# Modulation scale before shift, and the query product on scaled tokens, in a hybrid GLA/Hyena/MoE layer

## The chip, the cores and the metric

The kernel runs on one core of a Trainium2 chip. The metric is the device time in microseconds of one execution. Everything is float32.

## The reference, cut to what matters

One layer for a prompt of 128 tokens and a denoising sample of 256 tokens (384 tokens, width 2048). The first stage is the one that changes:

```python
mod = silu(cond) @ w_ada + b_ada            # w_ada: 2048 x 12288, two condition vectors
sh1, sc1, gt1, sh2, sc2, gt2 = split(mod, 6)
h = rmsnorm(x, g_pre_mix) * (1 + sc1) + sh1
proj = h @ w_in                             # columns: q 512, k 512, v 1024, g 1024, lr 32, Hyena 3072
la   = log_sigmoid(lr @ w_dec + b_dec) / 16 # decays of the gated linear attention, two directions
```

After that come gated linear attention over four heads, two long convolutions (Hyena), the output projection, a second norm and modulation with sh2 and sc2, a router, and sixteen experts of which each token uses two.

## The kernel before, in words

Each engine runs one fixed instruction list, written out by hand, and engines meet at semaphores. SyncE (SP) issues nearly all weight loads in one order; a load that waits for its buffer holds every later one back.

**Modulation.** `ada_step` (L439) takes 16 loads of 2 MB, each 128 rows of w_ada over the 4096 columns of shift and scale together, through three ring slots (`next_slot`, L333). It multiplies them by the silu of the conditions (`sT`) on four column groups of TensorE (L450). In between, `x_turn` (L456) transposes the normed tokens, and ScalarE copies them to `hT` (L1256). Then VectorE adds the bias row (`mod_row`, L1562), TensorE turns the row into columns (`mod_columns`, L479), and VectorE applies scale and shift to `hT` in 32 instructions (L1623), after which `project("q")` starts (L503, matmuls of 384 columns; L506 is the same function for 512).

**The order behind it.** q, the low-rank product lr (L532), eight decay products `la` (L541, each read by ScalarE at L1271 and by VectorE at L1632), k, v0, v1, the transposes of the decayed keys (L552), g0, g1, then six Hyena blocks, and the output projection. Every projection has two halves of one 2 MB load each.

**The other four rows of the modulation** are computed by VectorE, in pieces. A piece is 256 rows by 512 columns, loaded as two DMAs of 256 KB into the third ring slot, cut in four (`piece_view`). `run(n)` on VectorE works off n half pieces of two instructions each (L1587 for the first of a chunk, L1592 else). There are 16 chunks of 16 half pieces. When a chunk is complete, TensorE sums it over the partitions (`ada_sum`, L432) at the end of the projection half that the table `ADA_SUMS` names, and VectorE adds it to its row (`mod_chunk`, L1554). `PIECES_AFTER` says how many pieces SP loads behind which weight load; piece n waits until piece n-4 has been used.

**Where VectorE and TensorE meet.** Before the first attention head VectorE has run 136 half pieces: run(26), the eight decay rows L1632, run(4), the decay sums (L1640 to L1647), mod_chunk(0), run(14), the products with q and k (L1654 to L1659, "ks"), then mod_chunk(1), run(20), mod_chunk(2), run(16), mod_chunk(3), run(16), mod_chunk(4), run(20), mod_chunk(5), run(16), mod_chunk(6), run(4), mod_chunk(7). TensorE's side of a head (`gla_updates`, L564) is woven into the second half of g1. It writes a state update into one PSUM bank per direction and, before it writes the next, waits until VectorE has read the last (L1685, L1687).

Of the kernel before, what the change touches and what calls it, by code (L numbers as in the profile page):

```python
# [20 lines left out]
P = 128  # L21
D = 2048
# [39 lines left out]
def shape_constants():  # L62
# [15 lines left out]
    base = np.concatenate([ident, tri, sel.reshape(P, 2 * P), total, np.tile(rows, (P, 1)), tokens, lower], 1).astype(np.float32)  # L78
# [55 lines left out]
def build(nc, T):  # L134

    ctx = ExitStack()
    with ctx:
# [17 lines left out]
        base = sb("base", [P, 4 * P + 32 + N_ROWS + NT + 1])  # L155
# [5 lines left out]
        colA = sb("colA", [P, 50])  # L161
# [18 lines left out]
        second_half = base[:, at_row + N_ROWS + NT:at_row + N_ROWS + NT + 1]  # L180
        ps = ctx.enter_context(nc.psum_tensor("ps", [P, 8, NCOL], F32))
# [20 lines left out]
        rowsA = region(25856, P, rows=50)  # L202
# [36 lines left out]

        wr = at(AT_GAIN, KT, 32)  # L240
# [89 lines left out]
        def slot_view(slot):  # L330
            return ring_mem[:, SLOT * slot:SLOT * (slot + 1)]
# [19 lines left out]
        def w_block(w, row0, col0):  # L351
# [9 lines left out]
        ADA_BANK = 6  # L361
        ADA_KEYS = ["ada0", "ada1", "ada2", "ada3", "ada4", "ada5"]
# [4 lines left out]
        PIECES_AFTER = {1: 8, 2: 8, 3: 3, 4: 6, 5: 4, 6: 7, 7: 7, 8: 8, 9: 9, 10: 7, 11: 5, 12: 4, 13: 6, 14: 4,  # L367
                        15: 6, 16: 4, 17: 8, 18: 2, 20: 2, 22: 2, 24: 2, 25: 4, 27: 4, 28: 6, 29: 2}
# [38 lines left out]
        def _(pe):  # L407
# [4 lines left out]
            pe.wait_ge(S("in_rowsA"), 16 * 6)  # L412
            take(pe, 5, "colA")
            tr(ps[:, 5, 0:50], rowsA, ident[0:50, 0:50]).then_inc(filled("colA"), 1)
            pe.wait_ge(S("in_rowsB"), 32)
            take(pe, 4, "colB")
            tr(ps[:, 4, 0:96], rowsB, ident[0:96, 0:96]).then_inc(filled("colB"), 1)

            pe.wait_ge(S("in_mlp"), 16 * 9)
            take(pe, 3, "hid1")  # L420
            mm(ps[0:HID, 3, 0:TOK], w1s, pe_sb, start=True, stop=True).then_inc(filled("hid1"), 1)

# [14 lines left out]
            ada_at = [0]  # L437

            def ada_step():  # L439


                third, k = divmod(ada_at[0], KT)
                ada_at[0] += 1
                w = next_slot(pe, w_ada[k * P:(k + 1) * P, third * SLOT:(third + 1) * SLOT])
                for n in range(8):
                    bank, j = ADA_BANK + n // 4, n % 4
                    key = ADA_KEYS[third * 2 + n // 4]
                    if k == 0 and j == 0:
                        take(pe, bank, key)
                    m = mm(ps[32 * j:32 * j + 32, bank, :], sT[:, k, :], w[:, n, :], start=(k == 0),  # L450
                           stop=(k == KT - 1), skip_group_check=True)
                    if k == KT - 1 and n == 3:
                        m.then_inc(filled(key), 1)
                slot_done(m, key if k == KT - 1 else None)
# [8 lines left out]
            pe.wait_ge(S("sT_ready"), 2)  # L463
            for k in range(KT):
                ada_step()
                if k == KT - 8:
                    pe.wait_ge(S("hid_ready"), 1)
                    take(pe, 3, "hid2")
                    mm(ps[:, 3, 0:TOK], w2s, ftmp[0:HID, 1, :], start=True, stop=True).then_inc(filled("hid2"), 1)
                    pe.wait_ge(S("x_scaled"), NT)  # L470
                if KT - 8 <= k < KT - 1:
                    for kt in range(3 * (k - KT + 8), min(KT, 3 * (k - KT + 8) + 3)):
                        x_turn(kt)

# [6 lines left out]

            wait_read(pe, "dve", ADA_KEYS[0])
            mod_columns(0, 2)
            pe.wait_ge(S("mod_ready"), 1)
            mod_columns(1, 3)

            def project_half(key, kind, w, col0, kh, readers=("act",), between=None, banks=(0, 1, 2, 3),
# [4 lines left out]
                for m_ in range(n):  # L492
# [3 lines left out]
                    if m_ == 2 and between:  # L496
                        between()
                    for k in range(8):
                        kk = kh * 8 + k
                        if key == "q" and m_ == 0:  # L500
                            pe.wait_ge(S("h_modulated"), kk + 1)
# [24 lines left out]
            project("q", "fm", w_in, COL_Q)  # L526

            pe.wait_ge(S("in_lr"), 16)
            take(pe, 4, "lr", ("act",))
            for k in range(KT):  # L530
                j = k % 4
                m = mm(ps[32 * j:32 * j + 32, 4, 0:TOK], wlr[:, k, :], hT[:, k, :], start=(k < 4), stop=(k >= KT - 4),  # L532
                       skip_group_check=True)
            m.then_inc(filled("lr"), 1)

            wait_read(pe, "act", "lr")
            pe.wait_ge(S("in_dec"), 128)
            for d in range(2):
                for h in range(HEADS):
                    take(pe, 4 + h % 2, f"la{d}{h}", ("act", "dve"))  # L540
                    mm(ps[:, 4 + h % 2, 0:TOK], wdec[:, d, h * DK:(h + 1) * DK], lrT,  # L541
                       start=True, stop=True).then_inc(filled(f"la{d}{h}"), 1)
            project("k", "fm", w_in, COL_K)
# [192 lines left out]
            pe.wait_ge(S("mod_ready"), 3)  # L736
# [229 lines left out]
        def _(sp):  # L966

            def small_loads():
                sp.dma_start(rowsA[0:16, :], T["c_ctx"].rearrange("(k p) -> k p", p=P)).then_inc(S("in_rowsA"), 16)
# [5 lines left out]
                sp.dma_start(base[:, :], T["k_base"]).then_inc(S("in_base"), 16)  # L975

            pieces = [0]
# [13 lines left out]
            for i, (slot, src) in enumerate(loads):  # L991
# [66 lines left out]
        def _(pool):  # L1058
# [5 lines left out]
            g.op(nc.gpsimd.memset(wdec, 0.0), S("wdec_zero"))  # L1064
# [73 lines left out]
            pool.wait_ge(S("mod_ready"), 2)  # L1138
# [11 lines left out]
            pool.wait_ge(S("mod_ready"), 4)  # L1150
            pool.dma_start(prompt_gate.rearrange("o (j n) -> (o j) n", j=4), mod[0:P:32, 5, :]
                           ).then_inc(S("prompt_gate_row"), 16)
# [6 lines left out]
            pool.dma_start(br[:, NG:NG + NE], T["b_router_exp"].broadcast_to([P, NE])).then_inc(S("in_router"), 16)  # L1159

# [46 lines left out]
        def _(act):  # L1207
# [6 lines left out]

            load(rowsB[0:72, :], T["hy_conv_w"][0].rearrange("j (m p) -> (j m) p", p=P), "in_rowsB")
# [7 lines left out]
            for t in range(NT):  # L1223
                load(x_sb[:, t, :], x_rows[t], "in_x")
# [5 lines left out]

            act.wait_ge(S("sin_arg"), 1)
            a.op(A(ftmp[0:HID, 1, :], ftmp[0:HID, 0, :], ACT.Sin), S("hid_ready"))
# [12 lines left out]
            act.wait_ge(S("in_x"), 16 * NT)  # L1245
            for t in range(NT):
                squares(x_sb[:, t, :], h_tm[:, t, :], t)
            act.wait_ge(S("eps_ready"), 1)
            roots(0, NT, D)
            act.wait_ge(S("sin_arg"), 2)  # L1250
            a.op(A(hdn[:, :], ftmp[:, 0, :], ACT.Sin), S("hdn_ready"))

            def h_columns(name):
                for kt in range(KT):
                    b = read(act, f"{name}{kt}")
                    a.op(A(hT[:, kt, :], ps[:, b, 0:TOK], ACT.Copy), freed("act", f"{name}{kt}"))  # L1256

            h_columns("xT")
# [4 lines left out]

            for m_ in range(4):
                copy_out(f"q_{m_}", qf[:, m_, :])
# [242 lines left out]
        def _(dve):  # L1508
# [13 lines left out]
            v.op(ve.tensor_copy(colA[:, :], ps[:, b, 0:50]), freed("dve", "colA"))  # L1522
            b = read(dve, "colB")
            v.op(ve.tensor_copy(colB[:, :], ps[:, b, 0:96]), freed("dve", "colB"))
# [19 lines left out]
            dve.wait_ge(S("in_mlp"), 16 * 9)  # L1544
            sine_argument("hid1", 0, HID)

            def mod_chunk(m):

                if m == 0:
                    dve.wait_ge(S("in_rows"), 16 * 10)  # L1550
# [6 lines left out]
            def mod_row(q):  # L1557

                dve.wait_ge(S("in_rows"), 16 * 10)
                if q < 2:  # L1560
                    b = read(dve, ADA_KEYS[q])
                    v.op(ve.tensor_tensor(mod[:, q, :], mod[:, q, :], ps[:, b, :], ALU.add), freed("dve", ADA_KEYS[q]))  # L1562
                if q % 3 == 0:
                    return
# [575 lines left out]
```

## Time and profile before

| what | value |
|---|---|
| time, median of 3 runs | 1530.26 us (1526.99 to 1530.33) |
| the profiled execution: its time, its span | 1530.56 us, 1528.7 us |
| TensorE (PE) matmul busy | 1379.7 us, 90% |
| VectorE (DVE) busy | 748.8 us, 49% |
| ScalarE (ACT) busy | 241.7 us, 16% |
| DMA | 422.19 MB, mean 276 GB/s |
| chain that ended last | PE 74%, DMA 11%, DVE 8% |

TensorE, VectorE and DMA in 40 slices of 38 us (tenths of busy time; PEclk is the granted TensorE clock):

```profile
PE   2679999999999989999999999889989888798977
DVE  0139889998677687978693752530000000000006
PEclk9689999999999999999999999989999999999999
DMA  9998458777549643322215844589999999999996
```

The first three slices are the modulation. Up to slice 25 the layer's body follows, and behind it the experts, in which DMA is at nine tenths. One matmul of float32 leaves two records in the trace, so a projection half of 32 matmuls of 384 columns shows as 64 records.

### The profile page before, as it was taken

To read this page: it belongs to the slowest core of one execution; us is meant where nothing else is said; L and a number is where in the kernel's file an instruction comes from. 1 tells how busy PE (TensorE), PEld (TensorE's weight loads), DVE (VectorE), ACT (ScalarE), POOL (GpSimd) and SP (SyncE) were. 2 spreads that over 40 slices of the span, in tenths; PEclk is the share of its full clock that TensorE was granted. 3 is DMA by queue.
4 is the path that set the end of the run, shared out by engine and by line. 5 is a ranking of instruction groups with operands and counts; after the bars stand their busy time and mean duration, and the time that the engine had idled before them with its cause. 6 is when DMAs were issued, how large, how long until landed. Compare 5 with 4: busy or idle time off the path is not lost.

```text
span 1528.7 us, 14045 instructions
## 1 busy us (share of the span) xinstructions
PE 1379.7 (90%) x5198; PEld 630.9 (41%) x5198; DVE 748.8 (49%) x1269; ACT 241.7 (16%) x401; POOL 75.1 (5%) x126
## 2 busy tenths in 40 slices
PE   2679999999999989999999999889989888798977
PEld 0135544444555545555544444543333333333322
DVE  0139889998677687978693752530000000000006
ACT  2110320100011111211121101521111101111104
POOL 3010000000001000000000001000000000000001
PEclk9689999999999999999999999989999999999999
DMA  9998458777549643322215844589999999999996
GB/s 345 424 359 254 170 173 276 249 259 254 165 144 339 222 146 109 117 69 90 83 55 213 289 157 170 235 351 427 427 426 394 430 427 428 426 386 427 427 424 279
DMA packets 134032, 422.19 MB, mean 276 GB/s; under 512 B 10253, under 2 KB 76024, under 8 KB 116852
## 3 DMA queue, kind: packets, MB, share of 16 engines
q1 hardware_dynamic: 120292, 375.79, 64.3%
q0 software_dynamic: 7584, 33.38, 6.0%
q10 hardware_dynamic: 6096, 12.20, 2.2%
q8 instruction: 40, 0.66, 0.2%
q14 instruction: 20, 0.16, 0.0%
HBM read 407.96 MB, written 22.58 MB: 282 GB/s over the span
## 4 chain that ended last, share of the span: by engine, by line
PE 74%; DMA 11%; DVE 8%; issue 3%; ACT 2%; ACTq 0%; POOL 0%; DVEq 0%; SPq 0%; POOLq 0%
PE ps L503 19%; PE ps L506 19%; PE ps L892 13%; PE ps L912 7%; DMA s_mem<-in_w_exp_gate 4%; PE ps L777 3%; DMA s_mem<-in_w_ada 3%; DMA s_mem<-in_w_exp_down 2%; DVE s_mem L1766 2%; PE ps L450 2%; PE ps L674 1%; DMA s_mem<-in_hy_freq 1%; PE ps L625 1%; PE ps L432 1%; DVE s_mem L1738 1%
## 5 line engine op out<-in xcount | busy, mean ns | idle before, releaser
L1592 DVE SCALAR_TENSOR_TENSOR s_mem<-s_mem,s_sT 128x512 f32<-128x512 f32 x480 | 339.4, 748 | 32.6 <-DMA s_mem<-in_w_ada 16.2
L503 PE MATMUL ps<-s_mem 128*128 128x384 f32 x1024 | 342.5, 492 | 1.1 <-DVE s_mem L1623 1.1
L506 PE MATMUL ps<-s_mem 128*128 128x512 f32 x672 | 292.8, 594 | 0.7 <-ACT s_mem L1366 0.7
L892 PE MATMUL ps<-s_mem 128*64 128x512 f32 x1152 | 256.4, 602 | 19.9 <-DMA s_mem<-in_w_exp_gate 18.7
L503 PEld LDWEIGHTS ps<-s_mem 128*128 128x128 f32 x1024 | 193.3, 191 | 142.5 <-issue 18.0
L506 PEld LDWEIGHTS ps<-s_mem 128*128 128x128 f32 x672 | 126.3, 190 | 158.5 <-issue 157.6
L892 PEld LDWEIGHTS ps<-s_mem 128*64 128x64 f32 x1152 | 87.4, 139 | 185.9 <-issue 185.9
L2059 DVE TENSOR_TENSOR s_mem<-s_mem,ps 64x512 f32<-64x512 f32 x18 | 12.2, 679 | 296.3 <-ACT s_mem L1461 296.3
L912 PE MATMUL ps<-s_mem 128*64 128x512 f32 x576 | 144.2, 659 | 9.3 <-DVE s_mem L2061 9.3
L1262 ACT ACTIVATE s_mem<-ps 128x512 f32<-128x512 f32 (+1 forms) x61 | 34.4, 581 | 316.3 <-PE ps L506 154.0
L912 PEld LDWEIGHTS ps<-s_mem 128*64 128x64 f32 x576 | 43.7, 150 | 96.4 <-issue 84.6
L2066 DVE COPY s_mem<-ps 128x512 f32<-128x512 f32 x18 | 12.4, 691 | 141.9 <-PE ps L912 141.9
L450 PE MATMUL ps<-s_mem,s_sT 128*32 128x512 f32 x256 | 43.2, 815 | 20.5 <-DMA s_mem<-in_w_ada 20.5
L1461 ACT ACT_TABLE_LOAD x17 | 21.8, 1283 | 241.0 <-PE ps L892 241.0
L625 PE MATMUL ps<-s_mem 128*128 128x512 f32 x96 | 42.9, 596 | 0.7 <-ACT s_mem L1262 0.7
L777 PE MATMUL ps<-s_mem 128*128 128x512 f32 x96 | 41.5, 592 | 0.0
L902 PE MATMUL ps<-s_base,s_mem 64*128 64x64 f32 x72 | 11.9, 285 | 30.9 <-DVE s_mem L2059 30.9
L1466 ACT ACTIVATE s_mem<-ps 128x512 f32<-128x512 f32 x18 | 10.7, 596 | 155.1 <-PE ps L912 155.1
L1307 ACT ACTIVATE s_mem<-ps,s_colB 128x384 f32<-128x384 f32 x24 | 16.1, 670 | 118.5 <-PE ps L503 118.5
L1893 DVE TENSOR_TENSOR s_mem<-s_mem,ps 128x512 f32<-128x512 f32 x12 | 7.9, 684 | 48.0 <-PE ps L777 25.1
L1347 ACT ACTIVATE s_mem<-s_mem 128x512 f32<-128x512 f32 x24 | 14.5, 630 | 93.5 <-DVE s_mem L1751 93.5
L450 PEld LDWEIGHTS ps<-s_mem,s_sT 128*32 128x32 f32 x256 | 8.3, 134 | 49.3 <-DMA s_mem<-in_w_ada 30.6
(287 smaller groups left out, 1025.0 us busy)
## 6 DMA issues: line engine op xcount, KB each, us to landing
s_mem<-in_w_ada SPq DMA_DIRECT2D x256, 256.0 KB, 3.2
s_mem<-in_w_exp_gate SPq DMA_DIRECT2D x32, 2048.0 KB, 21.1
s_mem<-in_w_exp_up SPq DMA_DIRECT2D x32, 2048.0 KB, 25.4
s_mem<-in_w_exp_down SPq DMA_DIRECT2D x32, 2048.0 KB, 24.4
s_mem<-in_w_in SPq DMA_DIRECT2D x24, 2048.0 KB, 8.8
s_mem<-in_w_ada SPq DMA_DIRECT2D x16, 2048.0 KB, 12.5
s_mem<-in_w_out SPq DMA_DIRECT2D x8, 2048.0 KB, 8.2
y_slots<-s_mem ACTq DMA_DIRECT2D x34, 256.0 KB, 11.1
```

What stands on the lines that cost most here:

```text
L450: m = mm(ps[32 * j:32 * j + 32, bank, :], sT[:, k, :], w[:, n, :], start=(k == 0), stop=(k == KT - 1), skip_group_check=True)
L503: m = mm(ps[:, banks[m_], 0:TOK], v[:, k, m_ * P:(m_ + 1) * P], hT[:, kk, :], start=(kk == 0), stop=(kk == KT - 1))
L506: m = mm(ps[:, banks[m_], :], hT[:, kk, m_ * P:(m_ + 1) * P], v[:, k, :], start=(kk == 0), stop=(kk == KT - 1))
L625: mm(ps[:, bank, :], dft[:, table, :], src, start=True, stop=True).then_inc(filled(key), 1)
L777: m = mm(ps[:, bank, :], hT[:, kh * 8 + k, t * P:(t + 1) * P], last_w[kh][:, k, :], start=(kh + k == 0), stop=(kh * 8 + k == KT - 1))
L892: m = mm(ps[half, 0, :], hgT[:, kh * 8 + k, :], weights(e, 2 * kh + which)[:, k, :], start=(kh + k == 0), stop=(kh * 8 + k == KT - 1), ski ...
L912: m = mm(ps[half, 4 + n // 2, :], heT[:, 2 * kh + k, :], weights(e, 4 + kh)[:, k, n * NCOL:(n + 1) * NCOL], start=(kh + k == 0), stop=(kh ...
L1262: a.op(A(dst, ps[:, b, 0:n], func), freed("act", key))
L1307: a.op(A(hyT[:, m_, :], ps[:, b, 0:TOK], ACT.Identity, bias=colB[:, 72 + c:73 + c], scale=colB[:, 24 + c:25 + c]), freed("act", key))
L1461: A(sg, ps[BLK:2 * BLK, 0, :], ACT.Silu).then_inc(S("sg_ready"), 1)
L1592: v.op(ve.scalar_tensor_tensor(out=o, in0=w, scalar=scale, in1=o, op0=ALU.mult, op1=ALU.add), S("piece_used") if last else None)
L1766: v.op(ve.reciprocal(temps[4 + s], ps[:, b, :]), freed("dve", f"norm{ho}{s}"))
```

## The change

Scale and shift are computed one behind the other. The scale comes in eight loads (two halves of 1024 columns, four loads each), then the shift in eight loads of 2048 columns. The tokens are multiplied by the scale only, q is computed on these while the shift's loads arrive, and the shift's part of q (shift times W_q) is computed as a row and added by ScalarE as a bias. The shift is then added to `hT` (32 VectorE instructions, as before) for the other projections. There are four ring slots in this stage, and both halves of W_q have buffers of their own. x is loaded ahead of the small tensors. The lr product moves behind the first half of k, and the decay products stand between the parts of k's second half.

```diff
-            slot = i % RING if i < KT else (i - KT + 1) % 2
+            slot = (0, 1, 2, 3, 0, 1, 2, 3, 0, 1, 2, 3, 0, 1, 3, 0)[i] if i < KT else (i - KT + 1) % 2
...
-        ADA_SUMS = {("q", 1): 0, ("k", 1): 1, ("v0", 1): 2, ("v1", 0): 3, ("v1", 1): 4, ("g0", 0): 5, ("g0", 1): 6,
-                    ("g1", 0): 7, ("g1", 1): 8, ("hy00", 1): 9, ("hy01", 1): 10, ("hy10", 0): 12,
-        PIECES_AFTER = {1: 8, 2: 8, 3: 3, 4: 6, 5: 4, 6: 7, 7: 7, 8: 8, 9: 9, 10: 7, 11: 5, 12: 4, 13: 6, 14: 4,
+        Q_LOAD_AFTER = {3: 0, 7: 1}
+        ADA_SUMS = {("k", 1): 0, ("v0", 1): 1, ("v1", 0): 2, ("v1", 1): 3, ("g0", 0): 4, ("g0", 1): 5, ("g1", 0): 6,
+                    ("g1", 1): 7, ("hy00", 0): 8, ("hy00", 1): 9, ("hy01", 1): 10, ("hy10", 0): 12,
+        PIECES_AFTER = {16: 4, 17: 8, 18: 3, 19: 2, 20: 6, 21: 6, 22: 8, 23: 8, 24: 11, 25: 11, 26: 7, 27: 7, 28: 5,
...
+            def scale_columns(h):
+                wait_read(pe, "act", f"scale{h}")
+                take(pe, 5, f"scaleT{h}")
+                for i in range(8):
+                    m = mm(ps[:, 5, 32 * i:32 * i + 32], scale_sums[:, i % 4 * P:(i % 4 + 1) * P], conds[:, i // 4, :], ...)
+            def q_products(m_, kts):
+                for kt in kts:
+                    if m_ == 0:
+                        pe.wait_ge(S("h_scaled"), kt + 1)
+                    m = mm(ps[:, m_, 0:TOK], wq[kt // 8][:, kt % 8, m_ * P:(m_ + 1) * P], hT[:, kt, :], ...)
+            scale_step(0, 0)
+            scale_step(0, 1)
+            pe.wait_ge(S("x_scaled"), NT)
+            for kt in range(KT):
+                x_turn(kt)
+                if kt in (4, 9):
+                    scale_step(0, 2 + kt // 9)
+            scale_columns(0)
...
+            for m_ in range(4):
+                take(pe, m_, f"q_{m_}", ("act",))
+                m = q_products(m_, range(8))
+                scale_step(1, m_)
+            m.then_inc(S("q_read"), 1)
+            shift_step(0)
+            scale_columns(1)
+            shift_step(1)
...
+            for m_ in range(4):
+                m = q_products(m_, range(8, 12))
+                if m_ % 2 == 1:
+                    shift_step(2 + m_ // 2)
+            m.then_inc(S("q_read"), 1)
+            for m_ in range(2):
+                q_products(m_, range(12, KT)).then_inc(filled(f"q_{m_}"), 1)
+                shift_step(4 + m_)
+            shift_step(6)
+            shift_step(7)
+            q_products(2, range(12, KT)).then_inc(filled("q_2"), 1)
+            wait_read(pe, "dve", "shift")
+            mod_columns(SHIFT, 5)
+            q_products(3, range(12, KT)).then_inc(filled("q_3"), 1)
+            # 16 matmuls of 512 columns on four column groups: shift columns times W_q -> "qshift"
...
-            project("q", "fm", w_in, COL_Q)
+            project_half(*where_k, 0, between=q_shift_columns, banks=(4, 5, 7, 0))
+            # lr, 16 matmuls as before, in bank 3
+            project_half(*where_k, 1, banks=(4, 5, 7, 0), turn=decay_products())   # two la behind each quarter
...
 VectorE:
-            run(26)
+            run(12)
             for d in range(2):
                 for h in range(HEADS):
                     ...  # L1632, as before
-            run(4)
+                    if h % 2 == 1 and (d, h) != (1, 3):
+                        run(3)
+            run(6)
...
+            run(10)
             mod_chunk(1)
-            run(20)
+            run(10)
             mod_chunk(2)
...
-                    run((2, 1, 2, 1, 1, 1, 2, 2)[event])
+                    run((2, 2, 2, 1, 1, 1, 2, 2)[event])
...
-            mod_chunk(7)
             gla_head(0)
-            mod_chunk(8)
+            mod_chunk(7)
             gla_head(1)
             wait_read(dve, "act", "g1_2")
+            mod_chunk(8)
```

## Rows read from the trace of the kernel before

**Rows 1.** Windows of the whole core: busy us (instructions), clock, DMA share, GB/s.

```profile
core 0: us, PE busy (x) PEld busy (x) DVE busy (x) ACT busy (x) POOL busy (x), PEclk, DMA share, GB/s
0.00:105.80 105.80, 55.17 (x318) 15.82 (x319) 13.22 (x27) 18.76 (x30) 13.04 (x25) 0.85 0.95 379
162.00:360.00 198.00, 196.72 (x545) 92.57 (x543) 179.03 (x248) 30.64 (x34) 1.09 (x2) 1.00 0.70 228
26.00:31.00 5.00, 5.00 (x29) 1.30 (x32) 2.83 (x6) 0.52 (x1) 0.00 (x0) 1.00 0.84 318
640.00:642.00 2.00, 2.00 (x6) 0.76 (x4) 1.97 (x6) 0.60 (x1) 0.00 (x0) 1.00 1.04 407
```

**Rows 2.** Chain that ended last, in order of time: start us, us, what.

```profile
84.89 13.95 DMA s_mem<-in_w_ada
98.89 3.64 PE ps L450 x16
105.83 43.15 PE ps L503 x128
```

**Rows 3.** Timeline, TensorE, from lr to the first head.

```profile
149.72 2.82 PE L532 MATMUL ps<-s_mem 128*32 128x384 f32 x30
158.00 1.53 PE L541 MATMUL ps<-s_mem 128*128 128x384 f32 x4 [0.84 <-DVE s_mem L1632]
161.74 41.44 PE L503 MATMUL ps<-s_mem 128*128 128x384 f32 x128
203.11 1.06 PE L432 MATMUL ps<-s_mem 128*32 128x256 f32 x8
204.10 41.47 PE L506 MATMUL ps<-s_mem 128*128 128x512 f32 x96
366.07 0.70 PE L564 MATMUL ps<-s_mem 64*128 64x256 f32 x4
```

**Rows 4.** Timeline, VectorE, from the decay rows to the first head.

```profile
139.87 13.28 DVE L1592 SCALAR_TENSOR_TENSOR s_mem<-s_mem,s_sT 128x512 f32<-128x512 f32 x18
159.61 1.26 DVE L1632 TENSOR_SCALAR s_mem<-ps,s_colA 128x384 f32<-128x384 f32 x2 [1.11 <-ACT s_mem L1271]
169.72 1.76 DVE L1640 TENSOR_TENSOR s_mem<-s_mem 128x1536 f32<-128x1536 f32 x1 [0.55 <-ACT s_mem L1278]
183.73 0.41 DVE L1554 TENSOR_TENSOR s_mem<-s_mem,ps 64x256 f32<-64x256 f32 x1
209.38 0.19 DVE L1654 COPY s_decs<-s_mem 128x24 f32<-128x24 f32 x1 [4.88 <-ACT s_mem L1285]
219.84 0.41 DVE L1554 TENSOR_TENSOR s_mem<-s_mem,ps 64x256 f32<-64x256 f32 x1
361.67 0.42 DVE L1554 TENSOR_TENSOR s_mem<-s_mem,ps 64x256 f32<-64x256 f32 x1
363.40 0.76 DVE L1685 COPY s_mem<-ps 128x256 f32<-128x256 f32 x2 [1.31 <-PE ps L564]
```

**Rows 5.** The page's list of DMA issues: size, median us to landing.

```profile
s_mem<-in_w_in SPq DMA_DIRECT2D x24, 2048.0 KB, 8.8
```

**Rows 6.** Timeline, TensorE, ScalarE and VectorE in the first stage.

```profile
31.26 1.91 ACT L1237 ACTIVATE s_mem<-s_mem 128x2048 f32<-128x2048 f32 x1 [1.51 <-DMA s_mem<-in_x_sample]
79.44 1.92 PE L450 MATMUL ps<-s_mem,s_sT 128*32 128x512 f32 x16
104.09 0.66 PE L479 MATMUL ps<-s_base,s_mem 128*128 128x128 f32 x4 [1.03 <-DVE s_mem L1568]
105.01 9.87 DVE L1623 TENSOR_SCALAR s_mem<-s_mem,s_modT 128x128 f32<-128x128 f32 x32
114.80 0.87 DVE L1587 TENSOR_SCALAR s_mem<-s_mem,s_sT 128x512 f32<-128x512 f32 x2
```

**Rows 7.** Who waited for whom, VectorE from 100 to 1000 us: total, times, longest.

```profile
DVE s_mem L1592 <- DMA s_mem<-in_w_ada: 16.2, 9, 5.5
```

More of the change, by code:

```diff
@@ L77, in shape_constants @@
     lower = (np.arange(P) >= BLK)[:, None]
-    base = np.concatenate([ident, tri, sel.reshape(P, 2 * P), total, np.tile(rows, (P, 1)), tokens, lower], 1).astype(np.float32)
+    shifts = np.zeros((P, 32), np.float32)
+    for j in range(4):
+        for c in range(2):
+            shifts[32 * j + 2 + c, c] = 1
+    conds = np.zeros((P, 2, 32), np.float32)
+    for j in range(4):
+        for c in range(2):
+            conds[32 * j + c, j // 2, c] = 1
+    base = np.concatenate([ident, tri, sel.reshape(P, 2 * P), total, np.tile(rows, (P, 1)), tokens, lower, shifts, conds.reshape(P, 64)], 1).astype(np.float32)
     masks = np.zeros((P, 2, P), np.int32)
@@ L435, in ada_sum, with scale_step, shift_step @@
                 mi.then_inc(filled(key), 1)
[L437 to L454, printed above, removed]
+            def scale_step(h, r):
+                cols = SCALE * D + 2 * h * NCOL
+                w = next_slot(pe, w_ada[4 * r * P:4 * (r + 1) * P, cols:cols + 2 * NCOL].rearrange("(k p) n -> p k n", p=P))
+                if r == 0:
+                    take(pe, 7 - h, f"scale{h}", ("act",))
+                for kk in range(4):
+                    k = 4 * r + kk
+                    for jj in range(2):
+                        j = 2 * jj + k % 2
+                        m = mm(ps[32 * j:32 * j + 32, 7 - h, :], sT[:, k, :], w[:, 2 * kk + jj, :], start=(k < 2),
+                               stop=(k >= KT - 2), skip_group_check=True)
+                slot_done(m, f"scale{h}" if r == 3 else None)
+            def shift_step(a):
+                w = next_slot(pe, w_ada[2 * a * P:2 * (a + 1) * P, SHIFT * D:(SHIFT + 1) * D].rearrange("(k p) n -> p k n", p=P))
+                if a == 0:
+                    take(pe, 7, "shift")
+                for k in (2 * a, 2 * a + 1):
+                    for j in range(4):
+                        m = mm(ps[32 * j:32 * j + 32, 7, :], sT[:, k, :], w[:, 4 * (k % 2) + j, :], start=(k == 0),
+                               stop=(k == KT - 1), skip_group_check=True)
+                slot_done(m, "shift" if k == KT - 1 else None)
             def x_turn(kt):
@@ L461, in x_turn @@
                 m.then_inc(filled(f"xT{kt}"), 1)
[L463 to L473, printed above, removed]
             def mod_columns(q, bank):
@@ new lines, in _ @@
+            wait_read(pe, "dve", "shift")
+            mod_columns(SHIFT, 5)
+            q_products(3, range(12, KT)).then_inc(filled("q_3"), 1)
+            wait_read(pe, "dve", "modT0")
+            take(pe, 6, "qshift", ("act",))
+            for k in range(KT):
+                j = k % 4
+                m = mm(ps[32 * j:32 * j + 32, 6, :], sT[:, k, :], wq[k // 8][:, k % 8, :], start=(k < 4),
+                       stop=(k >= KT - 4), skip_group_check=True)
+            m.then_inc(filled("qshift"), 1)
@@ L487, in project_half, with q_shift_columns @@
+            def q_shift_columns():
+                wait_read(pe, "act", "qshift")
+                take(pe, 6, "colQ", ("act",))
+                for m_ in range(4):
+                    m = mm(ps[:, 6, m_ * 32:m_ * 32 + 32], q_shift[:, m_ * P:(m_ + 1) * P], shift_rows, start=True,
+                           stop=True, skip_group_check=True)
+                m.then_inc(filled("colQ"), 1)
             def project_half(key, kind, w, col0, kh, readers=("act",), between=None, banks=(0, 1, 2, 3),
@@ L495, in project_half @@
                         take(pe, banks[m_], bk, readers)
-                    if m_ == 2 and between:
+                    if m_ == (1 if key == "k" else 2) and between:
                         between()
@@ L1212, in load @@
                 act.dma_start(dst, src).then_inc(S(sem), 16)
+            for t in range(NT):
+                load(x_sb[:, t, :], x_rows[t], f"in_x{t}")
             load(rowsB[0:72, :], T["hy_conv_w"][0].rearrange("j (m p) -> (j m) p", p=P), "in_rowsB")
@@ L1249, in _, with sums_out @@
             roots(0, NT, D)
+            for kt in range(KT):
+                b = read(act, f"xT{kt}")
+                a.op(A(hT[:, kt, :], ps[:, b, 0:TOK], ACT.Copy), freed("act", f"xT{kt}"))
+            def sums_out(h):
+                b = read(act, f"scale{h}")
+                a.op(A(scale_sums, ps[:, b, :], ACT.Copy), freed("act", f"scale{h}"))
+            sums_out(0)
+            act.wait_ge(S("sin_arg"), 1)
+            a.op(A(ftmp[0:HID, 1, :], ftmp[0:HID, 0, :], ACT.Sin), S("hid_ready"))
+            act.wait_ge(filled("scaleT0"), uses["scaleT0"][2])
+            sums_out(1)
             act.wait_ge(S("sin_arg"), 2)
             a.op(A(hdn[:, :], ftmp[:, 0, :], ACT.Sin), S("hdn_ready"))
[L1253 to L1258, printed above, removed]
             def copy_out(key, dst, func=ACT.Copy):
@@ L1262, in copy_out @@
                 a.op(A(dst, ps[:, b, 0:n], func), freed("act", key))
+            copy_out("qshift", q_shift)
+            b = read(act, "colQ")
+            a.op(A(colQ[:, :, :], ps[:, b, 0:4 * 32].rearrange("p (m n) -> p m n", n=32)[:, :, 0:2], ACT.Copy),
+                 freed("act", "colQ"))
+            a.sync()
             for m_ in range(4):
-                copy_out(f"q_{m_}", qf[:, m_, :])
+                b = read(act, f"q_{m_}")
+                for c, toks in ((0, slice(0, SEQ)), (1, slice(SEQ, TOK))):
+                    a.op(A(qf[:, m_, toks], ps[:, b, toks], ACT.Identity, bias=colQ[:, m_, c:c + 1]),
+                         freed("act", f"q_{m_}") if c == 1 else None)
             copy_out("lr", lrT)
@@ new lines, in _ @@
+            inverse_roots(0, NT)
+            for t in range(NT):
+                v.op(ve.tensor_scalar(h_tm[:, t, :], x_sb[:, t, :], stat[:, t:t + 1], None, ALU.mult), S("x_scaled"))
+            scale_tokens(0)
+            b = read(dve, "colB")
+            v.op(ve.tensor_copy(colB[:, :], ps[:, b, 0:96]), freed("dve", "colB"))
+            dve.wait_ge(S("in_mlp"), 16 * 9)
+            sine_argument("hid1", 0, HID)
+            scale_tokens(1)
+            sine_argument("hid2", 1, P)
+            dve.wait_ge(S("in_rows"), 16 * 8)
```

184 lines of the change are left out of this document (106 added, 78 removed).

## The prediction

> **What bounds the kernel now.** I read the windows first. Up to 105.8 us DMA is 95% busy and TensorE 55.17 of 105.80; from 162 to 360 us TensorE is busy 196.72 of 198 and VectorE 179.03 of 198 [rows 1]. The chain shows the first stage waiting for w_ada: a load, 3.64 us of matmuls behind the last one, the turn of two rows into columns, then q with 43.15 us of TensorE [rows 2]. So the bytes set the first stage, and 43 us of matmuls that need none of the last bytes stand behind it. The timelines show what else hangs on it. TensorE has nearly no gap from k to the first head [rows 3]. VectorE is ready for that head at 362.08 (361.67 + 0.41), waits 1.31 us for TensorE's first state update, and TensorE issues the second at 366.07 [rows 3, 4]. Two engines thus arrive there together: TensorE with no slack to give, VectorE with 2 to 3 us.
>
> **That meeting decides the change.** It makes TensorE early. I count what each engine needs from one moment M, when the transposed shift row stands in PSUM.
>
> *The first stage.* Loads before the end of the shift stay at 16 of 2 MB; two of W_q join them. At 407 GB/s, the rate of such a load alone [rows 1], 2.10 MB take 5.15 us, together 10.3 us. Their bounds are 0 (gaps in the stream fill up) and 17.6 us (twice the 8.8 us to landing, latency and neighbours included [rows 5]); I take 10.3, since the stream is 95% busy. Four slots instead of three and a TensorE that no longer waits for the small tensors should close the gap at 26 to 31 us (share 0.84, [rows 1]): 1 to 1.5 us back. The last load landed at 98.89 [rows 2]; it will land at about 108.
> TensorE must keep up: 43.2 us of q, sixteen batches of 1.92 us and the turns. If x is squared by about 18 us (in the trace the squares begin at 31.26 and the scaled tokens follow 11.7 us later [rows 6]), x is scaled near 25 us, turned near 42, and q starts near 45. From there 41.4 (q, [rows 3]) minus its last two quarters of four k tiles (5.2), twelve batches (23.0) and about 3 us of columns end at 107 to 108. So TensorE and DMA arrive together, and neither has slack. The last batch costs 3.6 us (cold [rows 2]): 111.6. A piece of q (2.6) and four transposes (0.66 [rows 6]) give M = 115; bounds 109 (no gap, warm) and 123 (17.6 for the two loads, or TensorE late).
> ScalarE's bias copies, the sums' copies and the new small matmuls lie beside this stream or beside q. POOL's lr and decay loads wait for the first shifted tile as before, have over 20 us until lr, and its later memset of wdec (under 2 us) hides there.
>
> *TensorE after M:* last quarter of q's fourth block 2.6, the 32 records of shift times W_q 3.8 (twice 1.92, [rows 6]), so k starts at M + 6.6. Half of k 20.7, shift columns 0.7 (bounds 0.3 and 2, nearest are the four transposes of 0.66), lr 3.0, half of k 20.7, four pairs of decay products 6.1 (1.53 each, [rows 3]), a chunk sum 1.06: v0 starts at M + 58.9. In the trace it is 162.0 us from v0 (204.10) to the second state update (366.07), with the same five kinds of work in it. TensorE asks at M + 221 = 336. Alone, that would be 30 us earlier than before.
>
> *VectorE after M:* the shift row's copy and 32 additions 10.1 (copy 0.2, then 105.01 to 114.80, [rows 6]), so pieces start at M + 10.1 = 125; before, at 114.80. A half piece is 1.475 us (13.28 for nine, [rows 4]). run(12) with its cheaper first pair is 17.3, to M + 27.4. The first decay row now needs half of k, lr and a quarter: M + 36.2, and reaches VectorE 1.6 us later (158.00 to 159.61, [rows 3, 4]). VectorE idles 10.4 us. Then each pair of rows is 1.3, run(3) 4.4, and TensorE's next pair comes 6.7 later (5.2 + 1.5): 1.0 of waiting each. The fourth pair ends at M + 59.2. run(6) 8.9, decay sums with mod_chunk(0) 14.4 (169.72 to 184.14), run(14) 20.4 (to 204.50), and ks 10.5 (209.38 to 219.84) [rows 4]: M + 113.4. The wait of 4.88 us for ScalarE before ks goes, because k is copied earlier. From 219.84 to 362.08 it was 142.2 us; all of it stays, mod_chunk(7) moves away: 141.8. Of the DMA waits in pieces (16.2 us up to 1000 us, [rows 7]) I take 1 off, since five weight loads instead of six fall into that stretch; bounds 5 off and 5 on. VectorE is ready at M + 254.2 = 369.2.
>
> So 133 half pieces (136 before) begin 10 us later, and the idle time that the later lr and decay rows cost VectorE (13.4 us, before 5) eats what fewer pieces and the ScalarE wait give. TensorE asks at 336 and gets its answer at 369.6 (0.4 for VectorE's read of the first update), where it issued at 366.07: +3.5 us. In the head itself VectorE now runs two half pieces at event 1: its step is 2.9 + 0.9, TensorE's 3.4, and as VectorE is last, three steps cost 0.4 each: +1.3. Moving mod_chunk(7) and (8), the later sums and the load table behind piece 92 change nothing there: the counts of pieces before the same weight load are equal again (92, 96, 104), and the heads' sum of 180 half pieces too. The router's loads pass the prompt's gate row on POOL, with tens of microseconds to spare.
> Sum, against the profiled execution: 1530.56 + 3.5 + 1.3 = 1535.4, which is 5.1 above the median of the runs (the profiled run itself lies 0.3 above it).
>
> **The clock.** In the trace a batch of 16 records takes 1.92 us when TensorE has been at work and 3.64 after a wait for a load [rows 2, 6]; the granted clock is 0.85 up to 105.8 us and 1.00 in 162 to 360 [rows 1]. A stand of 30 us before the head would put its first step on the half clock: 3.4 us becomes up to 6.8, of which VectorE's 3.8 covers the first part, up to 3 us on top. I leave it out of the sum and in the range.
> The Trainium skill, TensorE: Matmul & The Clock Gate, section "HAM oscillation", says that waits for data put the engine back to half its clock, so that the next batch starts cold. The trace agrees, with 3.64 against 1.92 us. By it the continuous q stream would run warm, and the new stand would be paid by a cold restart, up to 1538.5.
>
> **The rivals.**
> *A, TensorE's lead survives.* If VectorE had room (49% busy over the span, idle times for DMA and PE), the head would start when TensorE asks: 366 - 336 = 30 us gained, less its own waits of 2 to 3 us for chunks: 1503. For it speaks that TensorE is 90% busy and on 74% of the chain. Against it: 179.03 of 198 us, and run() counts fix the order. It would need VectorE ready before 366, which takes more than 3 us out of its 254.2 or out of M; each further microsecond counts one for one. This is the one that ends on the other side.
> *B, the first stage comes late.* x arrives late, or batches and q run on the half clock, or W_q's loads cost 8.8 each; M = 123, and the meeting is at 377: 1543. For it: TensorE and DMA have no slack to each other there, and slots are freed only behind q blocks. Against it: q keeps the engine busy.
> *C, the chain gives some time back.* The new load table and fewer blocked pieces remove most DMA waits, or M is 110 or 111: +3.5 + 1.3 - 5, so 1530. For it: 16.2 us of such waits. Against it: five weight loads still fall between pieces.
>
> **How the numbers follow.** Forecast 0.53 (1535.4, told as 1535, own range 1530 to 1541), A 0.14, B 0.14, C 0.19. 0.3% is 4.6 us, what a measurement of this kernel can tell from no change. The forecast lies near that bound: 0.31 of it slower, 0.22 same. C: 0.16 same, 0.03 faster. That gives faster 0.17, same 0.38, slower 0.45. The range 1524 to 1543 leaves out A and a little at each end.
>
> **What would show it.** First-stage end (second step of additions) near 115 to 125; VectorE idle about 10 us before the first decay row; ks ready near 228; TensorE waiting about 30 us for VectorE at the state updates of the first head, near 340 to 370; from there every line shifted by the same few microseconds. No such wait, or one below 5 us, would prove the forecast wrong, and so would pieces that begin before 115 or after 135.

## The result, and the profile after

The changed kernel takes 1550.87 us (median of 4 runs, 1548.49 to 1552.58) against 1530.3 for the kernel before: ratio 1.0134, interval 1.012 to 1.0148. It is slower by some 20 us, where 5 were forecast. The profiled execution took 1548.49 us with a span of 1546.7, 18.0 more than before. Single times below are compared between profiled executions, one for each kernel. Such an execution can lie some way from its kernel's median: this one is 2.4 us under it, the furthest of those below are 4.8 under (e6) and 5.1 over (e5). I call a stretch in which TensorE only waits a stand.

The first stage did what the prediction said. This is the timeline of the changed kernel there, TensorE and VectorE: start us, duration, engine, line, operation, count of records, and in brackets the idle time before it and who ended it.

```profile
110.19 3.43 PE L465 MATMUL ps<-s_mem,s_sT 128*32 128x512 f32 x16 [2.80 <-DMA s_mem<-in_w_ada]
116.23 0.60 PE L480 MATMUL ps<-s_base,s_mem 128*128 128x128 f32 x4
117.12 8.84 DVE L1747 TENSOR_SCALAR s_mem<-s_mem,s_sT 128x128 f32<-128x128 f32 x32
122.92 5.43 PE L577 MATMUL ps<-s_mem 128*128 128x384 f32 x16
125.88 0.86 DVE L1681 TENSOR_SCALAR s_mem<-s_mem,s_sT 128x512 f32<-128x512 f32 x2
154.16 1.26 DVE L1755 TENSOR_SCALAR s_mem<-ps,s_colA 128x384 f32<-128x384 f32 x2 [11.13 <-ACT s_mem L1375]
```

The transposed shift row stands at 116.83 (116.23 + 0.60; forecast 115), k begins at 122.9 (forecast 121.6) and the pieces at 125.88 (forecast 125). VectorE then idles 11.13 us before the first decay row (forecast 10.4). These rows answer to [rows 6] and to the first decay row of [rows 4].

Between the decay rows and ks there are two waits that the kernel before didn't have. The same view, with ScalarE and with SP's DMA issues added:

```profile
174.07 1.28 ACT L1379 ACT_TABLE_LOAD   x1
174.81 8.87 DVE L1686 SCALAR_TENSOR_TENSOR s_mem<-s_mem,s_sT 128x512 f32<-128x512 f32 x12
175.36 3.00 ACT L1379 ACTIVATE s_mem<-s_mem 128x1536 f32<-128x1536 f32 x2
178.38 1.28 ACT L1382 ACT_TABLE_LOAD   x1
179.67 3.00 ACT L1382 ACTIVATE s_mem<-s_mem 128x1536 f32<-128x1536 f32 x2
182.58 1.61 ACT L1358 ACTIVATE s_mem<-ps 128x384 f32<-128x384 f32 x4
183.87 1.92 PE L439 MATMUL ps<-s_mem 128*32 128x256 f32 x8 [10.43 <-ACT s_mem L1358]
185.72 19.59 PE L580 MATMUL ps<-s_mem 128*128 128x512 f32 x42
206.53 1.42 DVE L1686 SCALAR_TENSOR_TENSOR s_mem<-s_mem,s_sT 128x512 f32<-128x512 f32 x2
207.91 0.37 SPq L1089 DMA_DIRECT2D s_mem<-in_w_in x1
208.32 16.08 SPq L1080 DMA_DIRECT2D s_mem<-in_w_ada x12
217.38 10.31 DVE L1686 SCALAR_TENSOR_TENSOR s_mem<-s_mem,s_sT 128x512 f32<-128x512 f32 x14 [9.43 <-DMA s_mem<-in_w_ada]
236.39 1.75 DVE L1784 TENSOR_TENSOR s_mem<-s_mem 128x1536 f32<-128x1536 f32 x1
```

Read it from the top. TensorE has finished k and stands 10.43 us at its first chunk sum, the matmuls of L439, until ScalarE, which is at the decays' Exp (L1379) and Ln (L1382) first, has copied k (L1358) out of PSUM; before, the answering sum at 203.11 had no wait [rows 3]. So v's first half ends late, about 207. SP issues the next weight load at 207.91, when that half has given its slot back, and the pieces stand behind that load in SP's queue, from 208.32. VectorE has used its last loaded piece by 208 and waits 9.43 us. It delivers ks at 238.14.

Then the first head (TensorE and VectorE; the third record is the step behind the wait):

```profile
378.60 0.76 DVE L1811 COPY s_mem<-ps 128x256 f32<-128x256 f32 x2
379.08 1.55 PE L645 MATMUL ps<-s_mem 64*128 64x256 f32 x4 [21.66 <-DVE s_mem L1811]
380.56 4.00 PE L580 MATMUL ps<-s_mem 128*128 128x512 f32 x6
384.49 0.70 PE L645 MATMUL ps<-s_mem 64*128 64x256 f32 x4
```

TensorE stands 21.66 us for VectorE (forecast: about 30) and issues the second state update at 379.08; before it was at 366.07 [rows 3], so 13.0 us of the 18.0 are there already. The windows (columns as in [rows 1]) show who was busy; the two lines answer to the first two of [rows 1]:

```profile
0.00:105.80 105.80, 80.48 (x426) 37.33 (x430) 18.06 (x55) 19.71 (x32) 11.08 (x22) 0.98 0.99 384
162.00:360.00 198.00, 178.77 (x468) 79.16 (x466) 175.00 (x243) 32.14 (x37) 1.09 (x2) 0.96 0.69 224
```

TensorE did 25 us more work in the first 105.8 us, and had 18 us less of it from 162 to 360 us; VectorE is at 175.00 of 198. The remaining 5 us follow the head: 2.0 in the head, 1.06 for a chunk sum that before lay ahead of the meeting, and 1.9 in small shifts, none above 0.7.

### The profile page after: what moved, and what is told of

The parts are those of the page before. It is cut to its first block, busy times and chain, and to the rows that moved or that the text cites. A ratio compares the mean times of both kernels' runs of the same rounds, so it can differ in the third digit from the quotient of the medians.

```text
span 1546.7 us, 14236 instructions
## 1 busy us (share of the span) xinstructions
PE 1387.4 (90%) x5266; PEld 637.8 (41%) x5266; DVE 754.7 (49%) x1302; ACT 243.8 (16%) x409; POOL 75.0 (5%) x124
## 4 chain that ended last, share of the span: by engine, by line
PE 65%; DVE 16%; DMA 13%; issue 3%; ACT 3%; SPq 1%; POOL 0%; DVEq 0%; ACTq 0%; POOLq 0%
PE ps L577 16%; PE ps L973 13%; PE ps L580 11%; DVE s_mem L1686 7%; PE ps L993 7%; DMA s_mem<-in_w_exp_gate 6%; DMA s_mem<-in_w_ada 5%; PE ps L497 3%; PE ps L858 3%; DVE s_mem L1892 2%; PE ps L755 1%; PE ps L706 1%; DMA y_slots<-s_mem 1%; DVE s_mem L1864 1%; PE ps L645 1%
## 5 line engine op out<-in xcount | busy, mean ns | idle before, releaser
L577 PE MATMUL ps<-s_mem 128*128 128x384 f32 x896 | 301.1, 492 | 0.0
L580 PE MATMUL ps<-s_mem 128*128 128x512 f32 x672 | 297.3, 601 | 0.7 <-ACT s_mem L1470 0.7
L1358 ACT ACTIVATE s_mem<-ps 128x512 f32<-128x512 f32 (+1 forms) x58 | 32.7, 587 | 306.9 <-PE ps L580 180.4
L497 PE MATMUL ps<-s_mem 128*128 128x384 f32 x128 | 45.4, 507 | 0.3 <-DVE s_mem L1720 0.3
L706 PE MATMUL ps<-s_mem 128*128 128x512 f32 x96 | 42.9, 596 | 0.7 <-ACT s_mem L1358 0.7
L858 PE MATMUL ps<-s_mem 128*128 128x512 f32 x96 | 41.5, 592 | 0.0
L645 PE MATMUL ps<-s_mem 64*128 64x256 f32 x80 | 15.5, 441 | 22.0 <-DVE s_mem L1811 21.7
L1411 ACT ACTIVATE s_mem<-ps,s_colB 128x384 f32<-128x384 f32 x24 | 16.1, 671 | 117.2 <-PE ps L577 117.2
L439 PE MATMUL ps<-s_mem 128*32 128x256 f32 x128 | 19.0, 423 | 17.3 <-ACT s_mem L1358 11.1
## 6 DMA issues: line engine op xcount, KB each, us to landing
s_mem<-in_w_exp_gate SPq DMA_DIRECT2D x32, 2048.0 KB, 21.2
```

The costliest lines, as they stand in the source:

```text
L497: m = mm(ps[:, m_, 0:TOK], wq[kt // 8][:, kt % 8, m_ * P:(m_ + 1) * P], hT[:, kt, :], start=(kt == 0), stop=(kt == KT - 1))
L577: m = mm(ps[:, banks[m_], 0:TOK], v[:, k, m_ * P:(m_ + 1) * P], hT[:, kk, :], start=(kk == 0), stop=(kk == KT - 1))
L580: m = mm(ps[:, banks[m_], :], hT[:, kk, m_ * P:(m_ + 1) * P], v[:, k, :], start=(kk == 0), stop=(kk == KT - 1))
L645: m = mm(ps[:, 4 + d, 0:DV], ksT[d][r:r + CHUNK, c // 2, h * DK:(h + 1) * DK], vtm[r:r + CHUNK, c // 2, h * DV:(h + 1) * DV], start=True, ...
L706: mm(ps[:, bank, :], dft[:, table, :], src, start=True, stop=True).then_inc(filled(key), 1)
L858: m = mm(ps[:, bank, :], hT[:, kh * 8 + k, t * P:(t + 1) * P], last_w[kh][:, k, :], start=(kh + k == 0), stop=(kh * 8 + k == KT - 1))
```

## The experiments

Each was compared with the kernel before, in 3 rounds on one chip (e1 to e4 together, e5 to e7 together). Theory 1 in all of them: VectorE's queue from its first piece to the first head sets the end, and the two waits above are what the prediction missed.

**e1, only the order of SP's loads.** Six pieces go ahead of v's next weight load.

```
-  19: 2, 20: 6, 21: 6, ...
+  19: 8, 21: 6, ...
```

> The changed kernel, with pieces 17 to 22 issued ahead of the load of v1's first half instead of behind it. Theory 1 (the chain to the first head runs through VectorE, and what I had not counted is its 9.4 us wait for piece 17, queued on SyncE behind a weight load whose slot TensorE frees late): the wait goes, TensorE's 10.4 us stand at the first chunk sum stays, time 1541 to 1542. Theory 2 (TensorE's stand at the chunk sum costs its own 10 us): time stays at 1551.

Measured 1547.56 us, ratio 1.0107 (1.0079 to 1.0135), which can't be told apart from the changed kernel's 1.0134 (1.012 to 1.0148). VectorE, and TensorE's first chunk sum, in this kernel:

```profile
183.97 1.92 PE L439 MATMUL ps<-s_mem 128*32 128x256 f32 x8 [10.43 <-ACT s_mem L1358]
227.16 1.75 DVE L1784 TENSOR_TENSOR s_mem<-s_mem 128x1536 f32<-128x1536 f32 x1
239.44 2.87 DVE L1686 SCALAR_TENSOR_TENSOR s_mem<-s_mem,s_sT 128x512 f32<-128x512 f32 x4 [3.14 <-DMA s_mem<-in_w_ada]
260.67 4.38 DVE L1686 SCALAR_TENSOR_TENSOR s_mem<-s_mem,s_sT 128x512 f32<-128x512 f32 x6 [3.68 <-DMA s_mem<-in_w_ada]
377.20 0.76 DVE L1811 COPY s_mem<-ps 128x256 f32<-128x256 f32 x2
```

ks comes 9.2 us earlier, but the wait for pieces comes back in five parts (3.14, 3.68 and three of 1.1 to 2.0), and the head gains 1.4 only. My 1541 to 1542 was a miss: TensorE was still 10 us late, weight loads are released by TensorE (here v's next one goes out at 215.32), and pieces queue behind one weight load or the next. This order of the queue only chose where VectorE pays.

**e2, only the order of ScalarE's work.** k is copied before the decay's Exp and Ln.

```
+  for m_ in range(4):
+      copy_out(f"k_{m_}", kf[:, m_, :])
   for d in range(2): ... ACT.Exp ...
   for d in range(2): ... ACT.Ln ...
-  for m_ in range(4):
-      copy_out(f"k_{m_}", kf[:, m_, :])
```

> The changed kernel, with ScalarE copying k out of PSUM before the exponentials and logarithms of the decays instead of behind them, so that TensorE's first chunk sum finds its bank free. Both theories: the 10.4 us stand goes and piece 17 comes in time, 1541 to 1542. If a third cause held piece 17 (the DMA queues), VectorE would still wait and the time stay at 1551.

Measured 1541.22 us, ratio 1.0071 (1.0046 to 1.0095): a hit. The same places in this kernel:

```profile
175.64 1.06 PE L439 MATMUL ps<-s_mem 128*32 128x256 f32 x8 [1.81 <-ACT s_mem L1358]
227.46 1.75 DVE L1784 TENSOR_TENSOR s_mem<-s_mem 128x1536 f32<-128x1536 f32 x1
371.46 0.76 DVE L1811 COPY s_mem<-ps 128x256 f32<-128x256 f32 x2
371.94 1.55 PE L645 MATMUL ps<-s_mem 64*128 64x256 f32 x4 [20.55 <-DVE s_mem L1811]
```

The chunk sum waits 1.81 instead of 10.43, no wait of VectorE for pieces before the head exceeds 1.5, and VectorE is ready 7.1 us earlier, at 371.46, close to the 369.2 that the prediction had. So copying k early gives back 9 to 10 us of the loss of 20 (7.1 of it at the head in the traces). What is left, 11.3 us over the kernel before where about 5 were forecast, has other causes; they stand with the prediction's steps below.

**e7, only the PSUM banks.** Is it ScalarE's late copy as such, or the bank? ScalarE still copies k last here.

```
-  project_half(*where_k, ..., banks=(4, 5, 7, 0))     (both halves)
-  project("v0", "tm", w_in, COL_V)
+  project_half(*where_k, ..., banks=(4, 5, 6, 0))     (both halves)
+  project("v0", "tm", w_in, COL_V, banks=(1, 2, 3))
```

> The kernel after with only the PSUM banks changed: k in banks 4, 5, 6 and 0 (was 4, 5, 7 and 0), the first half of v in banks 1, 2, 3 (was 0, 1, 2). ScalarE still copies k behind Exp and Ln. Theory 1 (TensorE's wait of 10.43 us at its first chunk sum, and the late load that starves VectorE of pieces for 9.43 us, come from k's third block standing in bank 7, which the chunk sums use, with v's first tile in bank 0 next): that wait falls below 2 us, VectorE's wait for pieces at 217 us below 4 us, and the time is that of the kernel with k copied first, 1541 us (1539 to 1543). Rival (ScalarE's late copies are what costs, by the decay products or by VectorE's wait for them before it multiplies k): the chunk sum's wait goes but the time stays at 1548 to 1551 us.

Measured 1542.7 us, ratio 1.0068 (1.0048 to 1.0088). TensorE behind the decay products, and the head:

```profile
175.96 1.06 PE L439 MATMUL ps<-s_mem 128*32 128x256 f32 x8
177.59 41.47 PE L580 MATMUL ps<-s_mem 128*128 128x512 f32 x96 [0.57 <-DMA s_mem<-in_w_in]
373.45 0.76 DVE L1811 COPY s_mem<-ps 128x256 f32<-128x256 f32 x2
373.93 1.55 PE L645 MATMUL ps<-s_mem 64*128 64x256 f32 x4 [21.59 <-DVE s_mem L1811]
```

The sum doesn't wait at all, and no wait for pieces above 1.7 us is left before the head. So the wait was for the bank: the change puts k's third block in bank 7, where all chunk sums go, and v's first tile in bank 0 behind k's fourth. That the head is 2.0 later than in e2 is the first stage's: the first decay row came at 156.76 here, 154.56 there. The ratios of e2 and e7 can't be told apart.

**e3, e2 and more.** Work for VectorE's idle 11 us as well: seven half pieces go from behind chunk 0's sum to ahead of the decay rows, and SP loads three pieces earlier.

```
-  19: 2, 20: 6,            +  19: 5, 20: 3,
-  run(12)                  +  run(19)      (ahead of the decay rows)
-  mod_chunk(0); run(14)    +  mod_chunk(0); run(7)
```

> As the second, with three more pieces ahead of v1's load and seven half pieces moved from behind the decay sums to before the first decay row, where VectorE idles 11.1 us. Theory 1 (VectorE's chain sets the first head): another 10 us, 1531 to 1532, about the time of the kernel before. Theory 3 (the rest of the loss, some 11 us, lies in the first stage or in TensorE's cold restart, not in VectorE's chain): 1541.

Measured 1535.62 us, ratio 1.0042 (1.0027 to 1.0056), between the two theories. VectorE, and then TensorE at the head:

```profile
153.95 1.26 DVE L1755 TENSOR_SCALAR s_mem<-ps,s_colA 128x384 f32<-128x384 f32 x2 [1.14 <-ACT s_mem L1375]
182.82 2.87 DVE L1686 SCALAR_TENSOR_TENSOR s_mem<-s_mem,s_sT 128x512 f32<-128x512 f32 x4 [5.29 <-DMA s_mem<-in_w_ada]
362.89 1.55 PE L645 MATMUL ps<-s_mem 64*128 64x256 f32 x4 [23.30 <-DVE s_mem L1811]
364.37 5.49 PE L580 MATMUL ps<-s_mem 128*128 128x512 f32 x6
392.09 1.06 PE L439 MATMUL ps<-s_mem 128*32 128x256 f32 x8
```

The idle time went from 11.12 (in e2) to 1.14, a piece came 5.29 late, and the head is 9.1 us earlier than in e2 and 3.2 earlier than before (362.89 against 366.07 [rows 3]). Yet the span is 5.0 longer than before, so 8.2 us are lost behind that point. Of these, 3.5 go in the head itself, behind the stand of 23.30: its first update and the step behind it take 6.90 us (362.89 to 369.79), where 3.41 are normal. By 392.09 the lead is gone (before, the sum that stands there began at 391.78). The extra chunk sum is 1.06, 2.6 come with a fall of the clock near 790 us (last section), and the last 1.0 is in small shifts. I had priced the head's landing, not what a stand costs after it.

**e4 and e6, half of VectorE's work on the pieces taken away.** In both kernels the pieces' instructions for the context condition are left out (all but the first of a chunk), so the last four modulation rows are not computed for it; e4 is e2 with these left out, e6 the kernel before with these left out.

```
   if c == 0:
       v.sync()
+      continue
```

> The changed kernel with ScalarE's early copy of k, and each half piece with one of its two instructions (the context condition's sums of the last four modulation rows are left out). VectorE then has 47 per cent less of this work. Theory 1: VectorE is ready long before the first head, TensorE does not stand there, and the whole lead of the first stage shows: head asked at about 342 us, time 1505 to 1510. Theory 3: the loss of the first stage stays, 1535 or more.

> The kernel before (not the changed one) with the sums of the context condition left out for the last four modulation rows: half of VectorE's instructions in its pieces go, their output is not the reference's. Control for the same cut in the kernel after, which gave 1503.96 us. Theory 1 (in the kernel before TensorE reaches the first head with no slack to give, so a free VectorE gains only TensorE's small waits for it): 1520 to 1529 us, so that 16 us or more of the 26 between the two is what the changed first stage is worth when VectorE isn't in its way. Rival (the cut itself is what gains, wherever it is made): 1503 to 1510 us, and the changed first stage is worth nothing.

Measured: e4 1503.96 us, ratio 0.9821 (0.9793 to 0.9849); e6 1522.02 us, ratio 0.9945 (0.9929 to 0.9962). e6 is a hit; e4 is 1 us under its 1505 to 1510, and TensorE still stood 2.89 us where none was expected. The second state update of the first head, first in e4 and then in e6:

```profile
343.46 1.03 PE L645 MATMUL ps<-s_mem 64*128 64x256 f32 x4 [2.89 <-DVE s_mem L1812]
```

```profile
363.28 0.70 PE L564 MATMUL ps<-s_mem 64*128 64x256 f32 x4
```

In the kernel before, a light VectorE brings the head 2.8 us earlier (363.28 against 366.07); 6.8 more it gains in the filter stage (from the chunk sum at 527.97 to that at 661.22 it is 133.25 us, before, from 530.76 to 670.83, 140.07). With the changed first stage the head comes at 343.46, 19.8 earlier than in e6. That is the lead which the change makes and which the kernel with all its pieces can't take. 6 us of it were lost again in e4's head, where two steps ran slow as in e3 (4.50 and 3.94 instead of 2.84, with a wait of 1.91 between them), 1.06 go for the extra chunk sum and 0.9 in small shifts, so in the profiled pair 12 us arrive at the end. The medians are 18.1 us apart (1522.02 and 1503.96, each on its own chip): e6's profiled execution was the fastest of its four, e4's the slowest.

**e5, the lead taken.** e3 with one chunk of pieces moved from ahead of the first head to the output stage. Nothing is left out. Each later chunk's sum moves one place back, and so do the areas in which the sums wait.

```
-  run(20); mod_chunk(5); run(16); mod_chunk(6); run(4)
+  run(20); mod_chunk(5); run(4)
   gla_head(0)
-  mod_chunk(7)
+  mod_chunk(6)                      ... and so on, one later each
   mod_row(4)
-  run(16)
+  run(24)                           (output stage; the rest behind it)
-  25: 11, ... 41: 4, 42: 6, 43: 2
+  25: 3,  ... 41: 8, 42: 8, 43: 4
```

> The kernel after with ScalarE's copies of k ahead of Exp and Ln, seven half pieces moved ahead of the decay rows, and one whole chunk of pieces (16 half pieces, about 24 us of VectorE) moved from before the first head to the output stage; all of the computation stays. Theory 1 (until the first head VectorE's queue sets the time, and TensorE has its lead ready): VectorE was ready for the first head at 362.41 us and will be near 338; TensorE asks near 342, so TensorE is last again, its stand of 23.3 us falls below 5, and the kernel takes 1505 to 1515 us, less than the kernel before. Rival (the pieces have no free place: what is taken away ahead of the head is paid back in the output stage or in the heads behind): the first head comes near 340 as well, but the end moves by less than half of it, 1522 to 1536 us.

Measured 1514.3 us, ratio 0.9887 (0.9871 to 0.9904): faster than both kernels by 1.1% and 2.4%. TensorE at the head, and at the end of the output stage:

```profile
344.87 1.03 PE L645 MATMUL ps<-s_mem 64*128 64x256 f32 x4 [2.76 <-DVE s_mem L1809]
895.31 22.56 PE L580 MATMUL ps<-s_mem 128*128 128x512 f32 x48 [2.56 <-DMA s_mem<-in_w_out]
917.80 1.06 PE L439 MATMUL ps<-s_mem 128*32 128x256 f32 x8
```

The stand of 23.30 is down to 2.76, and the head's second update lies 21.2 us earlier than before. The span is 11.1 shorter than before, so in this execution 10 us were given back, and not only in the output stage: 2.0 in the head, whose steps now go in VectorE's time (3.8 instead of 3.4), 1.5 for the extra chunk sum and what follows, 2.6 to a fall of the clock that e3 has as well (last section), and 4.2 in the output stage (821.66 to 917.80, 96.1 us; before 836.85 to 928.77, 91.9), where one chunk sum of 1.06 more falls, a wait of 2.56 for w_out, and 1.7 for the slower matmuls behind it (22.56 instead of 20.87), while a wait of 1.24 has gone. The rival is refuted: against e3 the head comes 18.0 earlier (344.87, 362.89), and 16.1 of it arrive at the end of the span. One part of theory 1 was a miss: TensorE still waits for VectorE, not the other way round. By the medians e5 gains 16.1 on the kernel before; its profiled execution was the slowest of four, and its first stage, the same code in all the changed kernels, ended late (the transposed shift row at 121.0, in e3 at 116.6).

The kernel before with a chunk moved in the same way was not run. e6 bounds what it could gain at the head: 2.8 us, with half of VectorE's work on the pieces gone.

## Why the prediction missed

Its sum was +4.8 on the profiled time; +18.0 was measured there. By its own steps:

- *M, the transposed shift row:* forecast 115, measured 116.83. q as filler and the cold last batch came as worked out (q from 45.20, forecast 45; the batch 3.43, forecast 3.6); the last load landed at 110.15 instead of about 108, and that makes the error of +1.8, within its bounds of 109 and 123. The seven executions with this first stage had M from 116.6 to 121.0, so a part of it is spread. Rival B (M = 123) didn't happen.
- *TensorE from M to its request:* forecast 336, with v0 starting at M + 58.9 right behind the chunk sum. It asked at about 357 (354.58 + 2.84). **This is the step that failed.** I put the chunk sum in with 1.06 us and no wait [rows 3] and never asked which bank it shares: k now stands in bank 7, and ScalarE copies it only behind two Exp and two Ln with their table loads. The wait was 10.43. Of the other 11, M is 1.8, waits for VectorE at two later sums are 4.9 (2.61 and 2.32), and the rest is slower steps behind each wait, such as 1.92 for this sum instead of 1.06.
- *VectorE from M to ks:* forecast M + 113.4, measured M + 121.3 (238.14). The 7.9 us are the wait for pieces (9.43) less small change. I gave waits for pieces 1 off, with bounds of 5 either way, from a row of before [rows 7]; it was 9.4 on in one place, as TensorE's stand held SP's queue (in all, waits for pieces before the head came to 12.8 us, before to 6.2). e2 and e7 take away the stand, by two different edits, and this wait goes with it: that the one makes the other is shown.
- *ks to the head:* forecast 140.8 (M + 113.4 to M + 254.2), measured 140.5. Right.
- *So the head:* forecast 369.6, measured 379.08: 1.8 + 7.9 - 0.2.
- *In the head:* forecast +1.3 by lockstep. In the changed kernel the lockstep cost nothing, because the cold first step (5.41 us from 379.08 to 384.49, before 3.41; granted clock 0.64 there) covered it: +2.0 by the clock, which I had left out of the sum. In e5, whose head ran at a granted clock of 1.00, the lockstep shows: steps of 3.8.
- *Behind it:* the prediction said that every line would be shifted by the same few microseconds. One chunk sum (1.06) had moved from behind q (before it stood at 148.91) to behind the meeting; I counted the sums before the head and not this one. 0.5 in the blocks behind the heads and 1.4 in small shifts have no cause that I tested.

So of the 13.2 us by which the profiled time missed, 7.9 are this failed step, by way of VectorE's wait; the rest is M, the cold step and what lies behind the head. The mechanism, two engines that meet at the first head with VectorE last, was right, and e4 with e6 shows it: taken alone, the new first stage is worth 19.8 us at the head. Rival A (1503) named what e4 then reached with a VectorE that had half to do. Rival C had it that pieces would be waited for less; they were waited for longer. On the clock the trace agrees with the rule that the prediction quoted from the Trainium skill, TensorE: Matmul & The Clock Gate, section "HAM oscillation": the step behind the stand of 21.66 us took 4.00 us instead of 2.84 and the update 1.55 instead of 0.70.

## What to carry to other kernels

When a change moves a tile to another PSUM bank, list who else uses that bank and when the tile's reader gets to it: here an unrelated small matmul of 1 us stopped TensorE for 10, and through the load queue starved an engine that has nothing to do with that bank. When the engine that leads is not the one that sets the end, give its lead away first (move work of the late engine behind the meeting): the same first stage cost 20 us as it stood and gained 16 in e5, which does that, fills VectorE's idle time as e3 does and takes the bank's wait away. The wait for loads, whose slots hang on another engine's stand, was not cured by the load table alone (e1).

## What the runs showed of the hardware

In these runs a long stand of TensorE cost more than its length. Behind the stands of 21.66 and 23.30 us the head's first update and the step behind it took 5.41 and 6.90 us instead of 3.41; e3's ran at a granted clock of 0.50, which is the lower level of 1.2 GHz. Behind the other three (e1 20.23, e2 20.55, e7 21.59) they took 6.73, 6.41 and 6.02, so the price, 2.0 to 3.5 us, doesn't follow the stand's length. In e4, which stood only 2.89 us, one step took 4.50 and the next 3.94 (granted clock 0.77 from 343.4 to 350.8); in e5, with 2.76 us, they took 2.84 (granted clock 1.00 from 344.8 to 349). So I can't say from these runs which stands bring the clock down. The granted clock of 360 to 470 us was 0.91 in the changed kernel.

The clock also fell far from any change. Three short rows of transposes stand between two long stretches of matmuls, near 790 us, and the 48 matmuls behind them took 20.87 us in the kernel before and in the changed one, but more in e3 and in e5. First before (its timeline, then a window with columns as in [rows 1]), then e3, then e5:

```profile
788.61 1.02 PE L716 MATMUL ps<-s_base,s_mem 128*128 128x128 f32 x6 [0.20 <-ACT s_mem L1366]
790.30 20.87 PE L506 MATMUL ps<-s_mem 128*128 128x512 f32 x48 [0.67 <-ACT s_mem L1366]
776.00:796.00 20.00, 16.57 (x63) 8.77 (x63) 19.72 (x33) 7.46 (x14) 0.00 (x0) 1.00 0.11 41
```

```profile
788.95 2.85 PE L797 MATMUL ps<-s_base,s_mem 128*128 128x128 f32 x12 [0.20 <-ACT s_mem L1470]
792.47 22.81 PE L580 MATMUL ps<-s_mem 128*128 128x512 f32 x48 [0.67 <-ACT s_mem L1470]
780.00:800.00 20.00, 17.42 (x50) 8.46 (x50) 19.69 (x32) 6.00 (x11) 0.00 (x0) 0.83 0.00 0
```

```profile
773.02 22.97 PE L580 MATMUL ps<-s_mem 128*128 128x512 f32 x48 [0.67 <-ACT s_mem L1470]
```

The waits and the work ahead are the same in all four, and the granted clock is 0.83 in e3's window and 1.00 in before's. The other five traces divide too: the time from the chunk sum ahead of this place to the one behind it is 166.0 us in e4, e6 and e7 as in the kernel before and the changed one, and 168.5 to 168.7 in e1 and e2 as in e3 and e5. So the clock fell in four of nine traces. With one trace for each kernel they don't show whether that goes with the kernel or with the execution, and why it falls is open; 2.6 us is half of what I had forecast for the whole change.
